# Head norms of the first mixer: column tiles, one root for four heads, row tiles

## The reference, cut to what matters

```python
def _rms_f32(xf):
    return xf * lax.rsqrt(jnp.mean(xf * xf, axis=-1, keepdims=True) + EPS)

def _l2norm(xf):
    return xf * lax.rsqrt(jnp.sum(xf * xf, axis=-1, keepdims=True) + EPS)
...
    q = _l2norm(q.reshape(bsz, s, h, d)) * (d ** -0.5)
    k = _l2norm(k.reshape(bsz, s, h, d))
```

## Time and profile before

| | |
|---|---|
| median of 3 runs | 1828.79 us (1828.6 to 1828.89) |
| profiled execution, its own time | 1830.11 us |
| its span | 1828.3 us |
| TensorE matmuls busy | 1781.8 us, 97% |
| VectorE busy | 1164.2 us, 64% |
| ScalarE busy | 722.9 us, 40% |

### The profile page before, as it was taken

The page is one execution under the profiler, slowest core; times in us unless marked ns, Lnnn a source line. Parts: engine busy times, 40 slices in busy tenths (PEclk is TensorE's granted clock), DMA queues, the critical chain, the costliest instruction groups (busy, mean ns, idle before and its releaser), DMA issues.

```text
span 1828.3 us, 23079 instructions
## 1 busy us (share of the span) xinstructions
PE 1781.8 (97%) x9356; PEld 1416.5 (77%) x9356; DVE 1164.2 (64%) x1684; ACT 722.9 (40%) x1028; POOL 0.2 (0%) x4
## 2 busy tenths in 40 slices
PE   8999989999999999999999999999997999999999
PEld 6867768788888888766788888888763788888887
DVE  5866743777777444667767777533898767777521
ACT  4246514644434333345544444322222644444311
POOL 0000000000000000000000000000000000000000
PEclk9999979999999999999999999999999999999999
DMA  6221101323222223211232322233563222232222
GB/s 228 93 69 61 56 21 32 118 95 102 95 94 97 95 95 104 83 43 35 88 108 93 103 93 92 94 99 107 159 166 108 70 95 101 92 104 90 95 96 78
DMA packets 56090, 171.27 MB, mean 94 GB/s; under 512 B 7848, under 2 KB 8360, under 8 KB 55856
## 3 DMA queue, kind: packets, MB, share of 16 engines
q1 hardware_dynamic: 55984, 169.80, 29.0%
HBM read 159.02 MB, written 2.10 MB: 88 GB/s over the span
## 4 chain that ended last, share of the span: by engine, by line
PE 86%; DVE 9%; ACT 3%; issue 2%; DMA 0%; SPq 0%; DVEq 0%; ACTq 0%
PE bank L179 85%; DVE conf_y L1162 3%; DVE wl L1154 1%; ACT mixer_arena L727 1%; DVE mixer_arena L1154 1%; DVE mixer_arena L1162 1%; ACT wh L727 1%; PE bank L612 1%; DMA raw<-in_w_in 0%; DVE conf_pad L1154 0%; DVE conf_u L1154 0%; DVE conf_y L1159 0%; DVE conf_val L1154 0%; ACT L727 0%; DVE conf_gate L1154 0%
## 5 line engine op out<-in xcount | busy, mean ns | idle before, releaser
L179 PE MATMUL bank<-nh,wh 128*128 128x512 f32 x1520 | 604.3, 398 | 11.5 <-DVE nl L1162 8.3
L727 ACT ACTIVATE wh<-raw 128x1024 fp32r<-128x1024 f32 (+2 forms) x310 | 309.0, 998 | 743.1 <-PE bank L179 733.6
L179 PE MATMUL bank<-nh,wl 128*128 128x512 f32 x1520 | 595.2, 392 | 0.0
L179 PE MATMUL bank<-nl,wh 128*128 128x512 f32 x1520 | 595.0, 391 | 0.0
L1154 DVE TENSOR_TENSOR wl<-raw,wh 128x1024 fp32r<-128x1024 f32 (+2 forms) x310 | 355.5, 1147 | 252.0 <-ACT wh L727 251.0
L179 PEld LDWEIGHTS bank<-nh,wh 128*128 128x128 f32 x1520 | 287.3, 189 | 80.1 <-issue 10.7
L179 PEld LDWEIGHTS bank<-nl,wh 128*128 128x128 f32 x1520 | 287.5, 189 | 61.3 <-issue 2.9
L179 PEld LDWEIGHTS bank<-nh,wl 128*128 128x128 f32 x1520 | 287.4, 189 | 60.8
L179 PE MATMUL bank<-ff_yh,wh 128*128 128x512 f32 x528 | 205.4, 389 | 0.0
L179 PE MATMUL bank<-ff_yh,wl 128*128 128x512 f32 x528 | 205.4, 389 | 0.0
L179 PE MATMUL bank<-ff_yl,wh 128*128 128x512 f32 x528 | 205.4, 389 | 0.0
(11 more groups left out here) (181 smaller groups left out, 1431.8 us busy)
## 6 DMA issues: line engine op xcount, KB each, us to landing
raw<-in_ff_a_up SPq DMA_DIRECT2D x44, 512.0 KB, 3.4
raw<-in_ff_b_up SPq DMA_DIRECT2D x44, 512.0 KB, 3.5
raw<-in_ff_c_up SPq DMA_DIRECT2D x44, 512.0 KB, 3.5
raw<-in_w_in SPq DMA_DIRECT2D x32, 512.0 KB, 3.5
raw<-in_pw SPq DMA_DIRECT2D x24, 512.0 KB, 3.6
conf_shifted<-conf_pad SPq DMA_DIRECT2D x128, 66.0 KB, 2.7
raw<-in_even_in SPq DMA_DIRECT2D x16, 512.0 KB, 3.5
raw<-in_ff_a_down_a SPq DMA_DIRECT2D x8, 512.0 KB, 3.5
```

What stands on the lines that cost most here:

```text
L179: return e.matmul(out, lhsT, rhs, start=start, stop=stop, skip_group_check=True)
L727: return e.activation(out, in_, func, **kw).then_inc(n.give(sem), 1)
```

## The change

Four heads' sums go into one bank: each of four matmuls uses 32 columns of ones and writes 32 rows, rows 32q to 32q + 31 for head q (`head_sums`). One logarithm and one exponential of 128 x 512 serve the four heads (`head_roots`). The factors then lie in 32 rows for each head, and TensorE spreads them to 128 rows: a matrix `leads` with ones in its rows 0, 32, 64 and 96, cut into four pieces of 32 rows, is multiplied with the same 32 rows of the factors, into banks 2 to 5 (`head_factors`). VectorE's scale reads the factor from the bank. `leads` is loaded as a part of `masks`.

```diff
-    def head_sum(i):
-
-        e.wait_ge(c.head_squared, i + 1)
-        if i >= 6:
-            e.wait_ge(c.head_logged, i - 5)
-        mm(bank[m1.sum_bank[i % 6]][:, :], c.ones[:, :], m1.hsq[i], True, True).then_inc(n.give(c.head_summed), 1)
+    def head_sums(g):
+
+        e.wait_ge(c.head_squared, 4 * g + 4)
+        if g == 2:
+            e.wait_ge(c.head_root, 1)
+        for q in range(4):
+            done = mm(bank[6 + g % 2][32 * q:32 * q + 32, :], c.ones[:, 0:32], m1.hsq[4 * g + q], True, True)
+        done.then_inc(n.give(c.head_summed), 1)
+
+    def head_factors(g):
+
+        e.wait_ge(c.mask_ready, 16)
+        e.wait_ge(c.head_root, g + 1)
+        if g:
+            e.wait_ge(c.head_scaled, 4 * g)
+        for q in range(4):
+            rows = slice(32 * q, 32 * q + 32)
+            done = mm(bank[2 + q][:, :], m1.leads[rows, :], m1.hsq[4 * g][rows, :], True, True)
+        done.then_inc(n.give(c.head_spread), 1)
...
         if i == 9:
             e.wait_ge(c.spread_used, HEADS)
-            for q in range(4):
-                head_sum(q)
+            head_sums(0)
         if i == 10:
             e.wait_ge(c.ret_copied, HEADS)
-            for q in range(4, 6):
-                head_sum(q)
+            head_factors(0)
+            head_sums(1)
         if i == 11:
-            for q in range(6, 12):
-                head_sum(q)
+            head_factors(1)
+            head_sums(2)
...
         piece(i % 2, c.nh, c.nl, range(DK))
+        if i == 0:
+            head_factors(2)
         if 1 <= i <= TB:
             t, cs = i - 1, slice((i - 1) * P, i * P)
             if t == 0:
-                e.wait_ge(c.head_logged, 12)
                 e.wait_ge(c.head_scaled, 12)
...
-    def roots_of(first, count, scale):
-        e.wait_ge(c.head_summed, first + count)
-        head_root(lambda q: bank[m1.sum_bank[(first + q) % 6]][:, :], lambda q: m1.hsq[first + q], c.head_logged, c.head_root,
-                  count, scale)
+    def head_roots(g, scale):
+
+        e.wait_ge(c.head_summed, g + 1)
+        act(m1.hsq[4 * g], bank[6 + g % 2][:, :], ACT.Ln, c.act_step, bias=c.eps[:, 0:1], scale=scale)
+        settle()
+        act(m1.hsq[4 * g], m1.hsq[4 * g], ACT.Exp, c.head_root, scale=-0.5)
...
             square_heads(m1.oret, 4)
+            head_roots(0, 1.0)
         if i == 10:
             square_heads(m1.gq, 8)
-            roots_of(0, 4, 1.0)
-        if i == 11:
-            roots_of(4, 2, 1.0 / P)
-
-    roots_of(6, 2, 1.0 / P)
-    roots_of(8, 4, 1.0)
+            head_roots(1, 1.0 / P)
+    head_roots(2, 1.0)
     feed()
...
     def head_scale(i):
-        e.wait_ge(c.head_root, i + 1)
-        x = (m1.gk, m1.oret, m1.gq)[i // 4][:, i % 4, :]
+        e.wait_ge(c.head_spread, i // 4 + 1)
+        x, factors = (m1.gk, m1.oret, m1.gq)[i // 4][:, i % 4, :], bank[2 + i % 4][:, :]
...
         if i == 11:
             for q in range(4):
                 head_scale(q)
     convolve(11)
+    for q in range(4, 8):
+        head_scale(q)
...
         if i == 0:
-            for q in range(4, 12):
+            for q in range(8, 12):
                 head_scale(q)
```

More of the change, by code:

```diff
@@ L125 @@
  ret_scored ret_weighed ret_done ret_copied decay_rows gcols_done gcols_ready spread spread_taken spread_used dec_ready decayed
- gdn_tap gdn_conv gdn_silu head_squared head_summed head_logged head_root head_scaled
+ gdn_tap gdn_conv gdn_silu head_squared head_summed head_root head_spread head_scaled
  chunk_ready chunk_used rg_silu gg_silu ret_mix ret_hi ret_low
@@ L777, in residual @@
                 chunk_split(i, k)
[L779 to L785, removed]
     def feed_forward(i, conv, bias):
@@ L1350, in head_scale @@
     def head_scale(i):
-        e.wait_ge(c.head_root, i + 1)
-        x = (m1.gk, m1.oret, m1.gq)[i // 4][:, i % 4, :]
+        e.wait_ge(c.head_spread, i // 4 + 1)
+        x, factors = (m1.gk, m1.oret, m1.gq)[i // 4][:, i % 4, :], bank[2 + i % 4][:, :]
         if i // 4 == 2:
-            stt(x, x, float(P) ** -0.5, m1.hsq[i], ALU.mult, ALU.mult, c.head_scaled)
+            stt(x, factors, float(P) ** -0.5, x, ALU.mult, ALU.mult, c.head_scaled)
         else:
-            tt(x, x, m1.hsq[i], ALU.mult, c.head_scaled)
+            tt(x, factors, x, ALU.mult, c.head_scaled)
     for i in range(12):
@@ L1940, in build @@
             pad=A[:, 35 * S:35 * S + 3 * (TAPS_GDN - 1 + S)].rearrange("p (k s) -> p k s", s=TAPS_GDN - 1 + S),
-            masks=A[:, 39 * S - 2 * P:39 * S], above=A[:, 39 * S - 2 * P:39 * S - P], below=A[:, 39 * S - P:39 * S],
+            masks=A[:, 39 * S - 3 * P:39 * S], leads=A[:, 39 * S - 3 * P:39 * S - 2 * P],
+            above=A[:, 39 * S - 2 * P:39 * S - P], below=A[:, 39 * S - P:39 * S],
             qd=slots(A, 39, 4), M=slots(A, 43, 4), qk=slots(A, 47, 4),
@@ L1945, in build @@
             rows=slots(A, 22), d=c.sq[:, 0, :].rearrange("p (t s) -> p t s", s=P),
-            hsq=[slots(A, i) for i in (19, 20, 21, 22, 16, 17, 4, 5, 12, 13, 14, 15)], sum_bank=(6, 7, 2, 3, 4, 5),
+            hsq=[slots(A, i) for i in (19, 20, 21, 22, 16, 17, 4, 5, 12, 13, 14, 15)],
             oret=slots(A, 0, 4), kbg=slots(A, 4, 4), kd=slots(A, 8, 4), vb=slots(A, 12, 4), gg=slots(A, 0, 4),
@@ L2016, in shape_constants @@
     out["causal"] = np.where(i[None, :] <= i[:, None], 0.0, NEG)
-    out["masks"] = np.concatenate([np.where(i[None, :] < i[:, None], 0.0, -NEG), np.where(i[None, :] >= i[:, None], 0.0, NEG)], 1)
+    out["masks"] = np.concatenate([np.repeat((i % 32 == 0)[:, None] * 1.0, P, 1), np.where(i[None, :] < i[:, None], 0.0, -NEG), np.where(i[None, :] >= i[:, None], 0.0, NEG)], 1)
     t = np.arange(16)
```

## The result

The median of five runs is 1839.74 us (1833.99 to 1843.23) against 1828.79 (1827.77 to 1828.97): a ratio of 1.0059, 95% interval 1.0045 to 1.0074. The kernel is slower, by 8 to 14 us. Five single executions far off their like (1998 to 7695 us; two of the kernel before, one each of three experiments) are left out of the medians, ranges and ratios of this document. The profiled execution is the longest of the five runs of the changed kernel: 1843.23 us with a span of 1841.4. Its block 9 ends 0.65 us later than before; in the profiles of the experiments that leave this place as it is, the same end varies from 166.1 to 170.6 us, so the 0.65 can't be put down to the change.

A forecast was written before the change was run, and what follows sets the result against it. TensorE was taken to bound the kernel; waits of 3.2 and 7.3 us and 2.1 us of low clock outweigh its cheaper sums, so +9.4 on 1828.79 gives 1838.2 us; range +8.2 to +10.6, with two rivals +6.4 to +12.6.

The forecast's parts named there:

- The groups of four: TensorE's head sums and spreads: four column tiles take 0.89 us, four row tiles 1.06, a change of shape 0.1.
- After block 9: TensorE's sums wait for all four squares, starting at 170.2, not 168.70; block 10 ends 1.0 us earlier.
- After block 10: TensorE's first spread waits 3.2 us for ScalarE's root of group 0, losing what was won before.
- After block 11: TensorE's second spread waits 7.3 us until VectorE has scaled heads 0 to 3 and so freed banks 2 to 5.
- fourth rival: Scales of heads 0 to 3 issued before VectorE waits for block 11: no change, 1828.8 us; 3%.
- The clock: TensorE runs at half rate after the 7.3 us wait behind block 11, which adds 2.1 us.
- Rival 2: The 3.2 us wait after block 10 lowers the clock too: another 2.1 us, +11.5, 1840.3 us; 25%.
- The total: Whole kernel: chunk stage starts at 211.7 against 202.29, +9.4 us, so a median of 1838.2 us.
- The range: Whole kernel: +8.2 to +10.6 us for the forecast itself, +6.4 to +12.6 with two of the rivals.
- rivals 1 and 2: TensorE's clock holds or recovers at once after block 11 (+7.3 us, 15%), or falls after block 10 too (+11.5, 25%).

The follow-up runs named there:

- e7_early_no_warm: Changed kernel with scales of heads 0 to 3 at i = 10 and of heads 4 to 7 before convolve(11), no idle work: 1827.29 us, ratio 0.9994.
- e1_scale_early: Changed kernel with VectorE's scales of heads 0 to 3 at i = 10 instead of 11: 1831.59 us, ratio 1.0013 to the kernel before.
- The two repeats: The changed kernel again, unedited, in two single executions: 1833.81 and 1835.42 us.
- e8_warm_a: Changed kernel with three idle-work matmuls in TensorE's wait after block 9: 1835.37 us, ratio 1.0041 to the kernel before.
- the second repeat: The second of two single executions of the unedited changed kernel: 1835.42 us.
- e5_shifted: Changed kernel with sums and spreads moved later, group 0's root before oret's squares, scales of heads 0 to 7 earlier: 1823.45 us, ratio 0.9978.
- e3_warm_bc: Changed kernel with three idle-work matmuls in the wait after block 10 and eight in that after block 11: 1835.88 us, ratio 1.0038.

## Why the prediction was right

**The groups of four.** 1.06 us was taken for the row tiles from a pair of 64-row ones, 1.07 is measured; 1.0 for the first group of sums with its change of shape, 0.99 measured. The drain at a change of tiling mode, of which the page TensorEngine Tiling (Array Packing) of the Trainium skill speaks in its section Key Properties, is in these numbers, and small: 0.1 us lies between the 0.99 here and the 0.89 of a group that follows its like the earlier trace rows.

**After block 9.** The group was forecast for 170.2, which is a wait of 3.2 us, and the end of block 10 for 1.0 us earlier than before. The wait is 3.27, block 10 ends 0.9 us earlier, counted from block 9's end, and the gain is lost again after block 10, as said. e7_early_no_warm shows the balance: 35.25 against 35.30.

**After block 10.** 3.2 us forecast, 3.11 to 3.20 measured where the clock had held before.

**After block 11.** 7.3 us forecast, 7.18 to 7.19 measured in five profiles; e1_scale_early shows that the cause is the place of four scales in VectorE's program. The forecast's fourth rival gave no change for just that edit. It overlooked that the spread of group 2 then waits for heads 4 to 7, 1.67 us, and the stretch stays 1.75 us above the 35.30 of before. With heads 4 to 7 earlier too (e7_early_no_warm) there is no change, with a ratio of 0.9994.

**The clock.** 2.1 us forecast behind the long wait, 1.5 to 2.7 measured. Rival 2, the drop after block 10, was given 25%. The profiled execution is that case. From the spread at 180.75 to block 11's scaling at 191.36 took 10.61 us; from 180.62 to block 11's end at 188.35 took 7.73 in e7_early_no_warm, and VectorE starts about 0.2 later: some 2.7 us where 2.1 was priced. With it the stretch grew by 12.4 us, against 11.5 for this rival. The two repeats without that cost have 8.7 and 9.1, against 9.4. So both cases of the forecast occur, and which one comes differs from execution to execution.

**The total.** 1838.2 forecast, 1839.74 measured. The 1.5 us between them can't be split from these runs, and with five executions spread over 9.2 us some luck is in so small a distance. The range was added up a little too narrow: three row groups and eight changes of shape stand behind the first root, and from the prices given they make +8.0 to +10.9, with rivals 1 and 2 +5.9 to +13.0. The measured +10.95 is at the edge of the first and inside the second. How often the clock falls after block 10 is open: in two of the four profiles that keep the wait of 3.1 us in full behind a block 10 at full clock (the changed kernel and e8_warm_a, not e7_early_no_warm and the second repeat). And the rest of the program differs by itself: from the chunk stage to the end of the span the profiles have 1621.3 to 1628.5 us, of the same TensorE work, and in the five of them that I took apart 79.7 to 84.7 of these lie between the start of the chunk stage and the end of its 64*64 matmuls (before 81.4, changed 80.7). The two repeats lie only 5.2 and 6.8 us above the 1828.6 of the kernel before in their set, though their stretches grew by 8.7 and 9.1: nearer the low end of the whole range than the forecast. Why the rest of the program differs is not shown.

## What to carry to other kernels

Cheaper matmuls on the busiest engine win only as far as nobody is late with their inputs: a group served by one instruction waits for its last member, and reused banks tie it to the reader of the group before. Before such a change, walk through the order of the engine that reads the result, from the last event that it shares with the matmul engine, and put the reader ahead of that event. Here this alone only brought the time of before back (e7_early_no_warm); the gain of 4 us came when the groups also stood a block later, so that their inputs were ready (e5_shifted). A wait of several microseconds should be priced with the low clock behind it, here a further 2 us on 7.

## What the runs showed of the hardware

Four float32 matmuls of 32 x 128 by 512 on four row tiles, into four banks, take 1.07 us together, where one matmul of 128 rows takes 0.86 (half of the pair's 1.72 in the earlier trace rows). At half clock the same group takes 2.02.

Waits of 3.1 to 3.3 us lowered TensorE's clock to the lower level (1.2 GHz) in some executions and not in others, for the same kernel and the same wait. That of 7.2 us did it each time. The waits of 1.0 to 2.6 us in this stretch left it at the upper level in each profile. So did the 7.2 us wait filled with matmuls whose result nobody reads (e3_warm_bc, one profile). For the filled short waits this proves nothing, since empty ones of the same length held the clock in other executions.
